# Stick-breaking attention: the mask put into the scores, one table set for exp and ln, another order on ScalarE, and unread products on TensorE

## What is computed

```python
mask = kpos[None, :] < qpos[:, None]
z = jnp.einsum('bhqd,bhsd->bhqs', qi, kh) * scale
log_beta = jax.nn.log_sigmoid(z)
log_rest = jnp.where(mask, jax.nn.log_sigmoid(-z), 0.0)
between = lax.cumsum(log_rest, axis=3, reverse=True) - log_rest
att = jnp.where(mask, jnp.exp(log_beta + between), 0.0)
return jnp.einsum('bhqs,bhsd->bhqd', att, vh)
```

## Time and profile before

| | us |
|---|---|
| median of 3 runs | 3406.39 |
| lowest, highest run | 3401.83, 3410.61 |
| the profiled execution | 3403.09 |
| its span in the profile | 3401.2 |
| TensorE busy (PE) | 3134.3 |
| VectorE busy (DVE) | 2227.4 |
| ScalarE busy (ACT) | 1608.8 |
| mean granted clock of TensorE | 0.952 |

### The profile page before, as it was taken

How to read it: one execution, slowest core, us unless ns; L and a number is a source line. 1 busy time by engine, 2 the same in 40 slices (tenths; PEclk the granted TensorE clock), 3 DMA queues, 4 the chain that set the end, 5 groups by cost and what they waited for, 6 DMA issues and landing times. The chain is left out here.

```text
span 3401.2 us, 47955 instructions
## 1 busy us (share of the span) xinstructions
PE 3134.3 (92%) x17334; PEld 2530.2 (74%) x17334; DVE 2227.4 (65%) x2810; ACT 1608.8 (47%) x1999; POOL 247.1 (7%) x192
## 2 busy tenths in 40 slices
PE   6888899899999888999979878799999999999996
PEld 5756688788877567888758656578888888888884
DVE  4375677336852266554555455489999899998995
ACT  1163333013233554100241343277777777777773
POOL 0000000000000000000000000021122211212211
PEclk9889899999999889999989889799999999999998
DMA  5410222222223000223652010599999999999994
GB/s 174 147 52 26 87 99 91 97 97 99 89 89 108 1 2 20 93 96 114 240 211 79 1 47 26 215 358 383 391 376 392 383 383 391 376 392 383 383 393 155
DMA packets 139146, 640.90 MB, mean 188 GB/s; under 512 B 13057, under 2 KB 54529, under 8 KB 79634
## 3 DMA queue, kind: packets, MB, share of 16 engines
q1 hardware_dynamic: 128754, 600.82, 46.6%
q0 software_dynamic: 9648, 35.13, 3.9%
q10 hardware_dynamic: 624, 3.29, 0.2%
HBM read 606.37 MB, written 32.56 MB: 188 GB/s over the span
## 5 line engine op out<-in xcount | busy, mean ns | idle before, releaser
L518 DVE TENSOR_TENSOR experts_rest<-experts_weights,experts_leading 128x2048 fp32r<-128x2048 f32 x386 | 878.6, 2283 | 80.7 <-ACT experts_leading L3619 79.2
L3619 ACT CAST experts_leading<-experts_weights 128x2048 fp32r<-128x2048 f32 x387 | 731.0, 1911 | 27.9 <-PEq L3609 16.6
L526 PE MATMUL psum<-experts_leading,experts_xT_rest 128*128 128x512 f32 x1024 | 399.8, 390 | 0.0
L525 PE MATMUL psum<-experts_rest,experts_xT_leading 128*128 128x512 f32 x1024 | 399.6, 390 | 0.0
L524 PE MATMUL psum<-experts_leading,experts_xT_leading 128*128 128x512 f32 x1024 | 399.3, 390 | 0.0
L525 PEld LDWEIGHTS psum<-experts_rest,experts_xT_leading 128*128 128x128 f32 x1024 | 192.7, 188 | 40.9
L526 PEld LDWEIGHTS psum<-experts_leading,experts_xT_rest 128*128 128x128 f32 x1024 | 192.7, 188 | 40.4
L524 PEld LDWEIGHTS psum<-experts_leading,experts_xT_leading 128*128 128x128 f32 x1024 | 193.0, 188 | 39.3
L524 PE MATMUL psum<-experts_leading,experts_hidden_leading 128*128 128x512 f32 x512 | 205.5, 401 | 0.0
L526 PE MATMUL psum<-experts_leading,experts_hidden_rest 128*128 128x512 f32 x512 | 200.5, 392 | 0.0
L525 PE MATMUL psum<-experts_rest,experts_hidden_leading 128*128 128x512 f32 x512 | 199.6, 390 | 0.0
(11 more groups left out here) (745 smaller groups left out, 6863.4 us busy)
## 6 DMA issues: line engine op xcount, KB each, us to landing
experts_weights<-in_w_up SPq DMA_DIRECT2D x259, 1024.0 KB, 9.4
experts_weights<-in_w_down SPq DMA_DIRECT2D x128, 1024.0 KB, 6.7
ada_unit<-in_w_ada SPq DMA_DIRECT2D x12, 2048.0 KB, 13.2
proj_weights<-in_w SPq DMA_DIRECT2D x15, 1024.0 KB, 4.8
proj_first<-in_w SPq DMA_DIRECT2D x14, 1024.0 KB
merge_first<-in_w_merge SPq DMA_DIRECT2D x16, 768.0 KB, 4.2
merge_weights<-in_w_merge SPq DMA_DIRECT2D x16, 768.0 KB, 4.1
ff_up_first<-in_w_up SPq DMA_DIRECT2D x11, 1024.0 KB, 4.8
```

The lines of the kernel that those rows point to most:

```text
L518: return dve.tensor_tensor(out, src, leading.bitcast(F32), ALU.subtract)
L525: pe.matmul(out, lh, rl, start=False, stop=False)
L526: return pe.matmul(out, ll, rh, start=False, stop=stop)
L3619: act.copy(leading[h % LEADING], weights.half(h)).then_inc(masked, 1)
```

## The change

The -1e30 of the mask is added by four products at the end of `scores` and no longer in `sums`, so that abs, exp and ln see it. The two multiplications on VectorE and the semaphore `soft_ready` go; `sums` waits for `added`. An instruction at the head of ScalarE's queue loads table set 6, which holds exp and ln. `logs` is split: `exps` (Abs and Exp) stays where it was, and `log` of head m+1 comes behind the weights' exp of head m. `unread(p, count)` issues products of 512 columns of the identity with Q into the PSUM bank that `values(p)` will overwrite; nobody reads them. Three stand ahead of sums(0), one behind sums(m) of each odd m. From the third pair on they wait for `taken`.

```diff
--- before.py
+++ after.py
@@ -1643,8 +1643,8 @@
         att = sb("att", [P, 4, COLS])
         later = sb("later", [P, 2, 3, P])
         f_rows = sb("forget", [H, T])
-        scored, absed, exped, logged, added, soft_ready, piled, summed, weighed, valued, taken = (sem(x) for x in (
-            "scores_ready", "magnitudes", "exps", "logs", "softplus_added", "softplus_ready", "later_tiles_added", "sums_ready",
+        scored, absed, exped, logged, added, piled, summed, weighed, valued, taken = (sem(x) for x in (
+            "scores_ready", "magnitudes", "exps", "logs", "softplus_added", "later_tiles_added", "sums_ready",
             "weights_ready", "values_summed", "results_taken"))
         x_back = sem("x_back")
         f_summed, f_copied, f_stored, f_spread = (sem(x) for x in ("forget_summed", "forget_copied", "forget_stored", "forget_spread"))
@@ -1674,22 +1674,29 @@
                     if m >= 2:
                         pe.wait_ge(weighed, m - 1)
                     for n in order:
-                        last = pe.matmul(tile(bank(m), n), keys[half, m // 2, n * P:(n + 1) * P], q[half, m // 2, n * P:T],
-                                         start=(n != 3), stop=True, skip_group_check=True)
+                        pe.matmul(tile(bank(m), n), keys[half, m // 2, n * P:(n + 1) * P], q[half, m // 2, n * P:T],
+                                  start=(n != 3), stop=True, skip_group_check=True)
+                    for n in order:
+                        last = pe.matmul(tile(bank(m), n)[:, 0:P], k.c("ident"), k.c("not_before"), start=False, stop=True,
+                                         skip_group_check=True)
                     last.then_inc(scored, 1)
 
                 def sums(m):
                     s, l = soft[:, m % 2, :], later[:, m % 2, :, :].rearrange("p a b -> p (a b)")
-                    pe.wait_ge(soft_ready, 2 * (m + 1))
+                    pe.wait_ge(added, m + 1)
                     for n in range(TT):
                         pe.matmul(tile(bank(m), n), k.c("minus_from"), tile(s, n), start=False, stop=True, skip_group_check=True)
-                        pe.matmul(tile(bank(m), n)[:, 0:P], k.c("ident"), k.c("not_before"), start=False, stop=True,
-                                  skip_group_check=True)
                     pe.wait_ge(piled, 3 * (m + 1))
                     for n, lo, hi, x in ((2, P, 2 * P, tile(s, 3)), (1, P, 2 * P, tile(s, 2, 0, P)), (0, P, 2 * P, tile(s, 1, 0, P)),
                                          (1, 2 * P, 3 * P, l[:, 2 * P:3 * P]), (0, 2 * P, 4 * P, l[:, 0:2 * P])):
                         last = pe.matmul(tile(bank(m), n, lo, hi), k.c("minus_ones"), x, start=False, stop=True, skip_group_check=True)
                     last.then_inc(summed, 1)
+
+                def unread(p, count):
+                    if p >= 2:
+                        pe.wait_ge(taken, p - 1)
+                    for _ in range(count):
+                        pe.matmul(k.bank(6 + p % 2), k.c("ident"), q[:, 0, :], start=True, stop=True)
 
                 def values(p):
                     pe.wait_ge(weighed, 2 * p + 2)
@@ -1712,14 +1719,18 @@
                 for m in range(heads):
                     if m + 1 < heads:
                         scores(m + 1)
+                    if m == 0:
+                        unread(0, 3)
                     sums(m)
-                    if m >= 2 and m % 2 == 0:
+                    if m % 2:
+                        unread(m // 2, 1)
+                    elif m >= 2:
                         values(m // 2 - 1)
                 values(heads // 2 - 1)
 
             @block.scalar
             def _(act):
-                def logs(m):
+                def exps(m):
                     x = mag[:, m % 2, :]
                     if m >= 2:
                         act.wait_ge(added, m - 1)
@@ -1727,17 +1738,24 @@
                     act.activation(x, bank(m), ACT.Abs).then_inc(absed, 1)
                     act.wait_ge(absed, m + 1)
                     act.activation(x, x, ACT.Exp, scale=-1.0).then_inc(exped, 1)
+
+                def log(m):
+                    x = mag[:, m % 2, :]
                     act.wait_ge(exped, m + 1)
                     act.activation(x, x, ACT.Ln, bias=k.c("one")).then_inc(logged, 1)
 
-                logs(0)
+                act.add_instruction(mybir.InstLoadActFuncSet(name=nc.get_next_instruction_name(), act_func_set_id=6))
+                exps(0)
+                log(0)
                 for m in range(heads):
                     if m + 1 < heads:
-                        logs(m + 1)
+                        exps(m + 1)
                     if m >= 4:
                         act.wait_ge(valued, m // 2 - 1)
                     act.wait_ge(summed, m + 1)
                     act.activation(att[:, m % 4, :], bank(m), ACT.Exp).then_inc(weighed, 1)
+                    if m + 1 < heads:
+                        log(m + 1)
 
             @block.vector
             def _(dve):
@@ -1749,11 +1767,6 @@
                         dve.wait_ge(summed, m - 1)
                     dve.scalar_tensor_tensor(s, bank(m), 0.0, mag[:, m % 2, :], ALU.max, ALU.add).then_inc(added, 1)
                     dve.wait_ge(added, m + 1)
-                    diagonals = s.rearrange("p (n c) -> p n c", c=2 * P)[:, 0:5:2, 0:P]
-                    dve.tensor_tensor(diagonals, diagonals, k.c("before")[:, 0:P].unsqueeze(1).broadcast_to([P, 3, P]),
-                                      ALU.mult).then_inc(soft_ready, 1)
-                    dve.tensor_tensor(tile(s, 3), tile(s, 3), k.c("before")[:, 0:P], ALU.mult).then_inc(soft_ready, 1)
-                    dve.wait_ge(soft_ready, 2 * m + 2)
                     if m >= 2:
                         dve.wait_ge(summed, m - 1)
                     dve.tensor_tensor(l[:, 2, :], tile(s, 2, P, 2 * P), tile(s, 3), ALU.add).then_inc(piled, 1)
```

## The result

| | before | after |
|---|---|---|
| median of 4 runs, us | 3406.97 | 3384.84 |
| lowest, highest | 3401.83, 3410.61 | 3378.72, 3390.46 |
| the profiled execution | 3403.09 | 3378.72 |
| its span | 3401.2 | 3376.8 |
| first score product to first product of the next stage | 99.51 | 79.18 |

The ratio of the runs is 0.9939, with a 95% interval of 0.9924 to 0.9954: faster, by 22.1 us between the medians. The last row but one is called the stretch from here on: 1087.71 to 1187.22 before, 1086.68 to 1165.86 after. It lies inside one execution, so the scatter of the rest of the kernel stays out of it. Each kernel was profiled once; how far the stretch itself varies from one execution to the next is not shown.

The account below looks back on a forecast made before the run. No engine full: a chain across ScalarE, VectorE and TensorE bounds the stage. Seven steps, together 60.23 us from W(0), move the last value products from 1183.79 to 1162.19: 3406.4 - 21.6 = 3384.8, say 3385; range 3378 to 3396.

Parts of the forecast that it names:

- Heads without values: From one weights' exp to the next, no value products ahead of the scores: 8.39 us a head.
- With values: From one weights' exp to the next, with value products ahead of the scores on TensorE: 9.30 us.
- The last: Step to the last head's weights' exp, no scores left, VectorE's max-and-add later than TensorE: 8.07 us.
- W(0): Start of head 0's weights' exp, behind three unread products and the sums: forecast at 1100.67 us.
- The load's cover: ScalarE idle 5.01 us ahead of the first abs hides the one remaining load's 1.28; uncovered, 1.3 once.
- Abs behind the joined mask: Scores to abs on TensorE and ScalarE, with four mask products added: 2.52 + 0.87 = 3.39 us.
- The clock: TensorE stays at 2.4 GHz; the head behind the 1.39 us idle may fall, bounds 0 and 6.6 us.
- clock at 1.00 from 1088 on: Sign of being right: TensorE's granted clock stays full from 1088 us on; 0.50 behind W(0) meant wrong.
- The bound from below: Max-and-add or scores (S) faster, as S(0) and S(1) together: 0.3 us in 8 heads, 2.4 more saved.
- Rival 1: Clock dips in one or two heads, 6.6 us each: saved 8.4 to 15.0, 3391 to 3398; chance 0.13.
- Rival 2: Compiler still places table loads in each ScalarE head: 65.6 instead of 60.2, saved 13.8, 3393; chance 0.04.
- Rival 3: TensorE, now the bound, at 1.2 GHz throughout: 26 us slower, 3432; chance 0.03.

Follow-up runs that it names:

- lean: Kernel before plus table load, unread products at the start, values head by head, mask off TensorE with VectorE zeroing the weights' diagonal blocks: stretch 75.35 us, median 3383.43.
- a_ln_first: Changed kernel with ln back right behind exp, ahead of the weights' exp: stretch 78.43 us, median 3384.60.
- a_fill_first: Changed kernel with one more unread product, behind sums(0), in the idle of 1.3 us: stretch 77.56 us, median 3382.96.
- a_no_table: Changed kernel without the explicit table load, so all 17 loads are back: stretch 92.64 us, median 3395.30.
- a_start_only: Changed kernel with only the three unread products ahead of sums(0), those behind odd heads left out: stretch 80.84 us, median 3391.79.
- a_split: Changed kernel with value products issued head by head instead of by pair, replacing odd heads' unread products, one unread behind sums(0): stretch 80.28 us, median 3384.93.

## Why the prediction was right

The forecast was 3385 us and 21.6 us saved; measured were 3384.8 and 22.1. Step by step:

- *Heads without values*: 8.39 worked out, 8.32 to 8.39 measured. *With values*: 9.30, and 9.23. *The last*: 8.07, and 7.91. *W(0)*: 12.96 behind the first scores, and 13.05. The mechanism is shown: the loads are gone, TensorE with the wait behind the weights' exp became the bound, and lean, with 0.87 us less for TensorE in a head, has heads shorter by 0.9.
- *The load's cover*: the one load stands at 1084.40, 5.8 us ahead of the first abs. It cost nothing.
- *Abs behind the joined mask*: 3.39 worked out, 3.61 measured. It is covered in the new order; in a_ln_first it is the 0.4 us a head.
- *The clock*: I took no loss behind the idle of 1.39 us and gave the bounds as 0 and 6.6. It fell, to 0.50 from 1103.1 to 1106.4, and cost 1.62 (a_fill_first). The sign "clock at 1.00 from 1088 on" failed, and the sign of being wrong, 0.50 anywhere behind W(0), showed, for 3.3 us. This is the term that was mis-sized: the first to the last value products took 75.74 us from the first scores where 74.48 were worked out, so the stage saved 20.3 and not 21.6.
- *The bound from below*: nothing of it came. S(0) and S(1), 4.04 us for both when they stood back to back, take 2.36 each in the changed kernel, with mask products behind each.
- *The rest of the span*: 24.4 us are missing from the profiled span, 20.3 of them in the stage. 1.0 lies ahead of it (first scores at 1087.71 and 1086.68), 3.0 behind it. I had put nothing there, and nothing of the change is there. Over the 14 profiled executions of this case the first scores lie between 1086.7 and 1095.0 us, with the same code ahead of them, and what follows the stage takes 2209.5 to 2218.7 us. That the median came within 0.2 us of the forecast is luck within this scatter; the stretch is what confirms the steps.
- *Rival 1*, the dips: one, at a quarter of the price of a whole slow head. *Rival 2*, loads that stay: they don't; made on purpose (a_no_table), its runs came to 3395 where 3393 was worked out. That is luck again: its stretch is 6.9 us shorter than before, where 13.8 was worked out, for the two ends of the stage and a fall of the clock, described above. *Rival 3* did not come: the changed kernel's stage is at 0.50 for 3.3 us, and not for a whole head.
- *What the working did not say*: it costed the four edits as one package and never asked what each does alone. The table load alone brings 17.2 us of stretch. The unread products alone bring 5.9, with the load 3.7 more (82.32 to 78.59). Mask and order on top of these make it 0.6 longer, and the mask alone costs 4.7. These are differences of one execution each, with falls of the clock in them: one of 3.3 us in the kernel with the load alone, which makes up most of the 3.7. The old order is bound by TensorE and the same wait too, once the loads are gone: 2.35 + 4.74 + 1.29 = 8.38 against ScalarE's 7.74, a sum that could be made from the earlier trace rows.

What stays open: why the fall of the clock comes behind one idle of 1.3 us and not behind another of the same length, and where the 8 us of scatter ahead of the stage come from. The first is not plain chance: ahead of the scores of head 2 an idle of 1.33 us was followed by a fall in all three kernels with the three unread products, the joined mask and no loads (the change, a_ln_first, a_start_only), and in only one (a_no_table) of the six where an idle of 1.96 us or more stood ahead of sums(0). For the second, the feed-forward products of the first block start anywhere from 360.8 to 368.6 us, so it is older than this stage.

## What to carry to other kernels

When a chain runs over two engines, write down both sums for one turn of the loop, with and without the cost that is to go: the larger one is what stays. Here that was TensorE's 8.38 against ScalarE's 7.74 once the loads were gone, and the mask and the order, two of the four edits, brought nothing that the stretches show. Count a table load by the step between its neighbours in the timeline (1.30 us), and look at the ends of the loop too, where it stands on the path again. An unread product in a wait is cheap insurance for the clock as long as it ends before the wait does, at 1.2 GHz as well.

## What the runs showed of the hardware

- *Idle and clock.* In the 14 profiles, of TensorE's idles of over 0.3 us ahead of score products (64 rows), none of the 21 up to 0.9 us was followed by a mean granted clock under 1.00 in the next 6 us, 8 of the 22 between 1.0 and 1.4 us were (0.63 to 0.72), and all 7 from 1.96 us up (0.50 to 0.72). Ahead of sums (128 rows) an idle of 1.86 us in the last head was followed by 1.00 in five of five, and one of 1.96 to 2.11 us ahead of sums(0) by 0.72 in five of five. The section A second HAM failure mode: psum-queue depth-cycling of the Trainium skill (TensorE: Matmul & The Clock Gate) says that short idles are enough for the clock to swing; the traces agree for 8 of the 22 between 1.0 and 1.4 us, and not for those below.
- *Two narrow products side by side.* Eight products with 64 columns of weights (x16 in the row), alternating between the two halves of the output's partitions, took 2.30 us; the four of one half alone took 2.30 as well (a_split). The Trainium skill (TensorE: Matmul & The Clock Gate, Why this matters for your kernels) says that outputs put at different column groups run at the same time; the trace agrees, and shows what is lost when the pairs are taken apart.
